# The order of VectorE's work in the attention steps of a conformer layer: taps behind the mix instead of ahead of it

## The reference, cut to what matters

```
h  = rms_norm(x);  z = h @ w_in            # columns: GLU a | GLU b | q | k | v | gate_conv | gate_attn
conv = w_conv_out( swish( layer_norm( depthwise_conv_31( a * sigmoid(b) ) ) ) )
attn = w_attn_out( rms_norm( (softmax(q1 k1) - lam * softmax(q2 k2)) @ v ) )   # 8 heads, chunk mask of 64
x  = x + ( sigmoid(gate_conv) * conv + sigmoid(gate_attn) * attn ) @ w_out
x  = x + peer( rms_norm(x) )               # top-k retrieval among 16384 single-neuron experts
```

## Time and profile before

| | before |
|---|---|
| median of 3 runs | 4130.09 us (4125.81 to 4134.25) |
| the profiled execution, its own time | 4123.05 us |
| its span | 4121.2 us |
| PE busy | 3856.9 us (94%) |
| PEld busy | 3796.5 us (92%) |
| DVE busy | 3128.3 us (76%) |
| POOL busy | 1370.9 us (33%) |
| ACT busy | 1057.1 us (26%) |
| granted TensorE clock, mean | 0.971 |

### The profile page before, as it was taken

The page is one execution under the profiler, slowest core; times in us unless marked ns, Lnnn a source line. Parts: engine busy times, 40 slices in busy tenths (PEclk is TensorE's granted clock), DMA queues, the critical chain, the costliest instruction groups (busy, mean ns, idle before and its releaser), DMA issues.

```text
span 4121.2 us, 68457 instructions
## 1 busy us (share of the span) xinstructions
PE 3856.9 (94%) x24995; PEld 3796.5 (92%) x24995; DVE 3128.3 (76%) x4305; ACT 1057.1 (26%) x1096; POOL 1370.9 (33%) x947
## 2 busy tenths in 40 slices
PE   8989989988999998999999999999989999999988
PEld 7889988988889998999999999999989999999988
DVE  6887888788766323578869999996788878888775
ACT  3222222222222112232233333332222212222211
POOL 3333333333334443566632222223133323333220
PEclk9999999999999999999999999999999999999999
DMA  7999989989978986876679999999698887888884
GB/s 279 317 345 320 321 304 340 340 296 335 345 258 294 347 310 230 286 264 234 240 266 383 387 381 386 386 380 392 247 338 306 310 313 299 323 304 300 319 304 147
DMA packets 451447, 1285.20 MB, mean 312 GB/s; under 512 B 34128, under 2 KB 258128, under 8 KB 343120
## 3 DMA queue, kind: packets, MB, share of 16 engines
q1 hardware_dynamic: 372336, 876.99, 60.2%
q0 software_dynamic: 46080, 335.56, 21.1%
q10 hardware_dynamic: 32832, 70.07, 4.4%
HBM read 1070.18 MB, written 345.75 MB: 344 GB/s over the span
## 4 chain that ended last, share of the span: by engine, by line
PE 42%; DVE 19%; issue 16%; DMA 13%; POOL 5%; SPq 3%; ACT 1%; DVEq 1%; POOLq 0%; ACTq 0%
PE ST L1734 16%; PE PA L1494 14%; PE ST L1824 8%; DMA w_raw<-w_all 6%; DMA u_rows<-u_out 6%; POOL w_lo L592 5%; DVE w_lo L1324 4%; DVE xg L1029 4%; DVE PA L1405 2%; DVE u_out L928 2%; PE ST L1799 2%; SPq L390 1%; DVE a_st L1365 1%; DVE acc L1391 1%; DVE wt_hi L1368 1%
## 5 line engine op out<-in xcount | busy, mean ns | idle before, releaser
L592 POOL TENSOR_TENSOR w_lo<-w_raw,w_hi 128x512 fp32r<-128x512 f32 x612 | 837.3, 1400 | 1225.5 <-ACT w_hi L647 1225.5
L647 ACT ACTIVATE w_hi<-w_raw 128x2048 fp32r<-128x2048 f32 x368 | 703.5, 1912 | 1452.3 <-PE ST L1824 669.6
L1824 PE MATMUL ST<-wt_hi,w_hi 128*128 128x384 f32 x2048 | 700.3, 342 | 80.3 <-DVE acc L1391 77.5
L1824 PE MATMUL ST<-wt_lo,w_hi 128*128 128x384 f32 x2048 | 696.5, 340 | 0.0
L1824 PE MATMUL ST<-wt_hi,w_lo 128*128 128x384 f32 x2048 | 695.7, 340 | 0.0
L1324 DVE TENSOR_TENSOR w_lo<-w_raw,w_hi 128x2048 fp32r<-128x2048 f32 x213 | 487.1, 2287 | 189.4 <-ACT w_hi L647 189.4
L620 POOL DMA_INDIRECT rows<-v_rows,v_idx x160 | 331.8, 2074 | 813.2 <-DVE PA L1405 787.0
L1494 PE MATMUL PA<-h_hi,w_hi 128*128 128x272 f32 x2496 | 547.0, 301 | 6.4 <-POOL w_lo L592 6.4
L1494 PE MATMUL PA<-h_hi,w_lo 128*128 128x272 f32 x2496 | 527.5, 294 | 0.0
L1494 PE MATMUL PA<-h_lo,w_hi 128*128 128x272 f32 x2496 | 527.4, 294 | 0.0
L1734 PE MATMUL ST<-h_hi,w_hi 128*128 128x384 f32 x1408 | 508.7, 361 | 2.6 <-ACT h_b L845 1.6
(11 more groups left out here) (270 smaller groups left out, 6237.5 us busy)
## 6 DMA issues: line engine op xcount, KB each, us to landing
w_raw<-w_all SPq DMA_DIRECT2D x368, 1024.0 KB, 6.8
u_in<-w_all SPq DMA_DIRECT2D x128, 1024.0 KB, 8.5
u_rows<-u_out SPq DMA_DIRECT2D x512, 256.0 KB, 7.4
v_rows<-w_all SPq DMA_DIRECT2D x128, 1024.0 KB, 9.1
a_scr<-gb ACTq DMA_DIRECT2D x128, 192.0 KB, 6.3
g_scr<-g_st ACTq DMA_DIRECT2D x24, 1024.0 KB, 11.7
a_st<-a_scr SPq DMA_DIRECT2D x15, 1536.0 KB, 8.4
gl_st<-g_scr SPq DMA_DIRECT2D x15, 1536.0 KB, 18.4
```

What stands on the lines that cost most here:

```text
L592: ins = pool.tensor_tensor(w_lo[:, slot, cols], raw[:, slot, cols], w_hi[:, slot, cols].bitcast(F32), ALU.subtract)
L647: act.activation(w_hi[:, slot, :], raw[:, slot, :], ACT.Copy).then_inc(hi_ready, 1)
L1824: last = mm(PD[k], a, r_[b][:, c, :], start=(c == 0 and y == 0), stop=(c == GRP - 1 and y == 2))
```

## The change

From step 2 on, VectorE's list has no taps between the maximum and the mix. The two taps that stood directly behind `glu` go too, and each step now has 9 taps instead of 8: five behind the mix, four behind the evacuation. The number of taps and of turns, and every instruction's operands, stay as they are. No other engine's list is edited.

```
                     glu(h, (r + 4) % 2)
-                    taps(h, 0, 2)
                     for s in range(2, STEPS):
-                        w = 2 + 8 * (s - 2)
+                        w = 9 * (s - 2)
                         att_max(g + s, s)
                         turn(hp, next(turns))
-                        taps(h, w, w + 4)
                         att_mix(g + s, s)
-                        taps(h, w + 4, w + 6)
+                        taps(h, w, w + 5)
                         turn(hp, next(turns))
                         evac(hp, r, s + 3)
-                        taps(h, w + 6, w + 8)
+                        taps(h, w + 5, w + 9)
                     if r == 0:
                         turn(hp, next(turns))
-                    taps(h, 2 + 8 * (STEPS - 2), TAPS)
+                    taps(h, 9 * (STEPS - 2), TAPS)
                     evac(hp, r, 8)
```

## The result

| | median | before, same runs | ratio, 95% interval |
|---|---|---|---|
| before | 4129.51 us (4125.81 to 4135.36, 6 runs) | | |
| changed | 4144.46 us (4136.92 to 4159.74, 6 runs) | 4129.51 us | 1.0048 [1.0033, 1.0062] |

The changed kernel is 15 us slower by the medians; the ratio, 1.0048, makes it 20 us, 14 to 26. Its profiled execution took 4136.92 us with a span of 4135.0, against 4123.05 and 4121.2: +13.8. All of it arises in the first stage: its last turn starts at 1170.64 instead of 1154.75, and from there to the end of the span are 2964.4 us, 2966.4 before. That execution is the fastest of the six, so what is read from its trace belongs to its own 14 us.

The account below looks back on a forecast made before the run. VectorE's gapless instruction list was taken to bound the first stage, holding TensorE. Three pairs at 5.1 us plus 4.8 plus 5.1 gave 25.2 us on 4130.1, so 4155 us; range 4116 to 4176, own range 4139 to 4178, slower 61%.

Parts of the forecast that it names:

- `o_norm` held less: Behind a head's last taps, `o_norm`'s instructions meet less of GpSimd's window: -2.1 us a first head, -0.5 a second.
- VectorE's waits for TensorE and `rstd`: These existing waits absorb lateness: -1.9 us in a second head, -2.25 at the start of the next pair.
- The store of step 2: The turn before step 2's mix, asked for earlier, waits 0 to 3.9 us for its buffer's store; 1.9 taken.
- the first window: GpSimd's first `w_lo` quarters in a head no longer fall on taps: -1.8 us a head.
- The groups of taps: Ten groups of taps a head become seven, losing three savings of 0.27 us semaphore turnaround: +0.8 us.
- The held taps: Five-tap pieces behind the mixes meet GpSimd's `w_lo` quarters: 11.0 us lost in three windows against 8.2, +2.8 a head.
- the fifth window: GpSimd's window behind unit 8 opens on taps still left: +3.2 us in a first head, +1.2 in a second.
- TensorE's waits: Waits for the mix at steps 2, 3, 4: 0.4, 6.1, 2.8 us, against 6.35, 2.38, 2.98 before.
- The end of the stage: The first stage's last turn, now behind five taps, comes 5.1 us later in its head; nothing behind absorbs it.
- rival 1: TensorE sets the pace and the earlier mix frees it: much faster, 4042 us at most; chance 4%.
- Rival 3: No difference: store waits and TensorE's lateness at pair starts absorb the windows' cost, 4130 to 4138 us; chance 17%.
- Rival 2: Somewhat faster through GpSimd's windows, if a five-tap piece loses under 2.5 us: 4105 to 4115, say 4110; chance 18%.

Follow-up runs that it names:

- two_seven: The changed kernel with 2 taps between mix and turn and 7 behind the evacuation, instead of 5 and 4: 4132.98 us, ratio 1.0021 to the kernel before.

## Why the prediction came true, and where its sizes were off

The forecast was slower, 4155 us in a range of 4116 to 4176; it is slower, 4144.46. The mechanism is shown: the half that builds the five-tap piece is +14 us alone, the taps are not held where GpSimd's windows are taken away, and laying turn and evacuation into the window, with the wait for the store as it is, turns the loss into a gain. Its size was put at 25 us and came out at 15 to 20.

For the sum I added up VectorE's busy and idle time by line up to the start of the stage's last turn, in both traces, and set the differences beside the prediction's terms for the same stretch (8 heads, the last one cut at that turn). The predicted column adds up to 25.0; 25.2 is the prediction's own rounding. The held taps are +8.4 here and +5 in the table of the experiments, because this sum leaves out the 2.6 us of the kernel before that are held behind its last turn and counts the overlap of two neighbouring instructions once.

| term | predicted us | measured us |
|---|---|---|
| waits of turns for stores | +15.2 (8 x 1.9) | +16.7 |
| turnaround between taps (fewer groups) | +5.3 | +3.7 |
| taps held by GpSimd | +26.9 | +8.4 |
| `o_norm` held less | -9.9 | -6.7 |
| VectorE's waits for TensorE and `rstd` | -12.5 | -9.5 |
| not in the prediction (`rope`, small operations of the mix) | 0 | +3.3 |
| sum, start of the last turn | +25.2 | +15.9 |

- **The store of step 2** was priced from the middle between 0 and 3.9 us. The eight waits are 1.8 to 2.6 us, 17.3 in all; that the middle came so close is luck. The other turns' waits changed by -0.6 together. This is the largest term; what pays for most of it is that the first window has no taps any more.
- **The groups of taps** were counted as ten that become seven. The lists have eleven that become seven in a first head and ten that become six in a second, so four turnarounds are lost and not three; each costs less idle time than was taken, and the term came out at +3.7 instead of +5.3.
- **The held taps are the mis-sized term**, with two parts. In windows 2 to 4 I predicted 11.0 us a head. It is 9.6 in first heads and 10.4 in second (3.1, 2.9, 3.6 and 3.6, 2.9, 3.9; predicted 3.4, 3.2, 4.4). The other and larger part is the fifth window: +3.2 in a first head and +1.2 in a second were predicted, 1.2 and 0.1 measured. The step that failed is "TensorE now comes to the end of unit 8 about 2.5 us earlier". Its hook in that unit now waits for `sq`, in seven of the eight heads and for 17.1 us, and behind the longest of these waits its clock is low. The chain is VectorE's own: the evacuation behind the held five taps is late (456.73, 58.3 us behind `glu`, where it was 55.0), ScalarE's work on it (L696) too, and `sq` (L742) stands behind that in ScalarE's order, up to the hook's start at 459.59:

```profile
457.44 0.66 ACT L696 ACTIVATE zb<-zb 128x544 f32<-128x544 f32 x1 [8.89 <-DVE zb L956]
...
458.88 0.66 ACT L742 ACTIVATE sq<-oraw 128x544 f32<-128x544 f32 x1
```

  So the window opens 67.5 to 71.7 us behind `glu` in first heads, where 66.9 was predicted and 69.4 is what every head had before. In the third head, with a wait of 1.5 us, the window does hit the taps and costs 2.9, close to the prediction; in the fifth, with no wait, it opens at 67.6 and costs 1.9; in the first and the seventh, with 3.1 us of wait, it opens at 71.7 and 70.8 and costs nothing. There the granted clock is at half behind the wait. Five us from the hook on, in the first head and in the third:

```profile
175.00:180.00 5.00, 4.76 (x17) 4.29 (x18) 4.78 (x7) 2.19 (x3) 0.00 (x0) 0.50 0.92 340
459.60:464.60 5.00, 5.00 (x36) 4.84 (x37) 4.71 (x8) 2.65 (x3) 0.00 (x0) 1.00 0.98 337
```

  With it the window opens 8.9 us (first head) and 9.2 us (seventh) behind the start of the hook, and without it 6.2 to 6.3 us (third, fifth), so the clock puts it off by about 2.8 us more. An engine that is held up also makes the window late that would have held it again.
- **The first window** lost its 1.8 us a head, as said: the first piece is held by the second window only.
- **TensorE's waits** were predicted at 0.4, 6.1 and 2.8 us for steps 2 to 4 of the third head: 0.92, 5.46 and 2.93. The low clock moved with them, by the busy times in three stretches behind the waits (PEclk third from the end):

```profile
407.00:412.00 5.00, 5.00 (x37) 4.26 (x37) 4.40 (x9) 2.30 (x2) 2.11 (x2) 1.00 0.94 298
427.00:432.00 5.00, 5.00 (x30) 5.00 (x31) 4.42 (x8) 2.40 (x2) 1.50 (x2) 0.69 1.01 409
446.00:451.00 5.00, 5.00 (x30) 4.93 (x29) 4.57 (x8) 2.09 (x3) 2.38 (x2) 0.66 0.97 289
```

  Step 2 has the full clock now, and the low one stands behind step 3, where the kernel before had 1.00 (427 to 432). Behind step 4 the mean is 0.66, as it was before the change (0.67 in 446 to 451). No experiment prices the clock alone; the trace has only the 2.8 us above.
- **The end of the stage**: from the last `glu` to the last turn are 58.1 us instead of 53.1, +5.1 as predicted, and nothing behind it takes that up.
- **"What counts is how long that list takes, and not when the mix comes in it"** was right as a reason against rival 1, and too strong as a rule: the moment of the mix sets the moment of the window. two_seven moves the mix ahead of its four taps and keeps two behind it, and gains and loses by windows that come elsewhere and by waits for stores.

Of the signs named, the piece of five taps takes 7.9 to 9.1 us, the waits at steps 2 and 3 are as said, and VectorE's evacuations wait twice for TensorE. `glu` to the last tap is 70.8 in the mean of the first heads, where 71 or more was said, and the fifth window meets taps in two of the four. Two readings of the prediction were off without changing its sum: TensorE's waits in the kernel before are not all for the mix (5.8 us are for `sq`), and its own range ends at 4178, where its terms give 4167.

Rival 1 (TensorE sets the pace, 4042 us) falls by its number. Its premise failed too: the waits for the mix shrank by 23 us, and those for `sq` grew by 27. Rival 3 (no difference) falls by the interval. Rival 2 put the turning point at a loss of 2.5 us for the piece between mix and turn. No window on a five-tap piece is under that. In the splits of three and four taps the windows are, and those kernels are faster. The lock that the Trainium skill describes ("SBUF — State Buffer", section Who interferes with whom) is seen here in kind. In size the rows stay below the 5.4 us a window that the prediction worked out for it: no window cost more than about 4.

The 3.3 us that the prediction didn't have are operations that GpSimd's windows now meet more often: a multiplication of `rope` (line 965) takes 3.3 us more in all, and so does the small product of the mix on line 1001, of which 11 instead of 8 instructions last 1.24 us instead of 0.15; the others together give 3 us back.

What stays open: whether three or four taps is the better split is not told by these runs (4115.39 and 4121.15 us, but the last turn starts at 1144.8 and 1136.2), nor why the two halves of the change don't seem to add.

## What to carry to other kernels

When one engine leads and another's work is triggered by it, an edit of the leader's order moves the other's window as well: look at which instructions the window will then lie on, and put there those that it does not hold. A wait of the busiest engine that disappears proves nothing if another engine has no hole in its list; here it came back at other hooks. Follow the chain round: here the held engine delayed the next window, which took back a large part of the predicted loss.

## What the runs showed of the hardware

- VectorE's taps and GpSimd's subtractions take turns, one instruction each. One row of the changed kernel's timeline each, of three tap instructions (32, 512 and 32 columns; the row prints the form of the first) and of two of GpSimd's quarters, inside a window:

```profile
410.50 4.19 DVE L1029 SCALAR_TENSOR_TENSOR xg<-u,params_sb,xg 128x32 f32<-128x32 f32 x3
...
411.67 2.98 POOL L592 TENSOR_TENSOR w_lo<-w_raw,w_hi 128x512 fp32r<-128x512 f32 x2
```

  Single instructions of this stretch: a 32-column instruction lasts 1.26 to 1.27 us instead of 0.25, about as long as a quarter; a 512-column one 1.59 instead of 0.75; GpSimd's quarter behind a 512-column one 1.74 to 1.82 instead of 1.28. The short instruction of a tap loses 1.0 us and the long one 0.8, so a tap that is split in 512 and 32 columns pays twice.
- The block transpose (2.30 us inside a window and outside) and the evacuation with one operand in PSUM (0.68) are not held at all, in any of the kernels. An instruction on one SBUF tensor can be held: the TENSOR_SCALAR on 128x2 of line 990 lasts 0.17 us elsewhere and mostly 1.04 in a window.
- Moving 2.9 us of such work by one tap (1 us) is worth 23 us of 4144 (five taps against four), as much as the whole change and more.
- Of the four waits of 3.1 us at the `stats` hook of unit 8, the granted clock was 0.50 (1.2 GHz) over the 5 us behind three and 1.00 (2.4 GHz) behind the fourth, at 605.35; it was 1.00 behind the waits of 1.5 and 1.8 us.
